# Expert stage of a two-block network: both halves of the tokens in one stationary tile, down weights taken straight from their landing buffer

## What is computed

```
def hierarchical_moe(h, w_rg, b_rg, w_re, b_re, w1, w3, w2):
    ...
    combine = jnp.sum(jax.nn.one_hot(expert_id, N_EXPERTS, dtype=jnp.float32)
                      * weight[..., None], axis=1)
    ...
        hid = jax.nn.silu(jnp.einsum('td,edf->tef', tk, w1)) * jnp.einsum('td,edf->tef', tk, w3)
        hid = hid * c[:, :, None].astype(hid.dtype)
        return jnp.einsum('tef,efd->td', hid, w2)
```

## Time and profile before

| | us |
|---|---|
| median of 3 runs | 1795.31 (1793.7 to 1795.73) |
| the profiled execution | 1794.04 |
| its span in the profile | 1792.0 |
| PE busy in the span | 1533.0 |
| DVE busy | 947.2 |
| ACT busy | 714.4 |
| expert stage, first token tile scaled to the last store's issue | 702.54 to 1062.24 |

### The profile page before, as it was taken

One profiled execution on the slowest core, in us unless ns is written; L12 is line 12 of the kernel. 1 busy time (PEld: TensorE's weight loads), 2 busy tenths in 40 slices (PEclk: granted clock), 3 DMA queues, 4 the chain that ended last, 5 costly groups with the idle time before them and its releaser, 6 DMA issues.

```text
span 1792.0 us, 17556 instructions
## 1 busy us (share of the span) xinstructions
PE 1533.0 (86%) x7159; PEld 1154.2 (64%) x7159; DVE 947.2 (53%) x1295; ACT 714.4 (40%) x1035; POOL 61.9 (3%) x64
## 2 busy tenths in 40 slices
PE   5999998779879954999999965984888798999999
PEld 4888876567547823555555534763877676678887
DVE  3443335834683445788888846745635353321334
ACT  4333143434453212666666643434212136652231
POOL 1000000000000001111111010000000000000000
PEclk9999999979889975999999987986989899999999
DMA  6422321022104323999999963200000222002241
GB/s 200 160 95 83 105 95 53 12 77 76 54 12 144 141 94 113 316 335 331 333 336 334 334 214 125 92 24 0 1 0 1 71 94 94 1 1 71 94 141 47
DMA packets 79179, 219.81 MB, mean 123 GB/s; under 512 B 8899, under 2 KB 10037, under 8 KB 74998
## 3 DMA queue, kind: packets, MB, share of 16 engines
q1 hardware_dynamic: 71670, 193.73, 32.0%
q0 software_dynamic: 4864, 16.52, 2.8%
q10 hardware_dynamic: 2560, 8.39, 1.3%
HBM read 197.91 MB, written 20.71 MB: 122 GB/s over the span
## 4 chain that ended last, share of the span: by engine, by line
PE 61%; DVE 25%; ACT 10%; issue 2%; DMA 1%; SPq 0%; POOL 0%; DVEq 0%; POOLq 0%; ACTq 0%
PE PS L497 15%; PE PS L499 14%; PE PS L498 14%; DVE wlo L1109 6%; DVE htlo L1109 5%; PE PS L892 4%; ACT whi L1881 3%; PE PS L494 2%; DVE ylo L1109 2%; PE PS L1034 2%; ACT yhi L1881 2%; ACT hthi L1881 2%; ACT work L1881 1%; PE PS L1025 1%; DVE work L1506 1%
## 5 line engine op out<-in xcount | busy, mean ns | idle before, releaser
L1109 DVE TENSOR_TENSOR wlo<-raw,whi 128x2048 fp32r<-128x2048 f32 x74 | 169.3, 2291 | 390.0 <-ACT whi L1881 390.0
L1881 ACT ACTIVATE whi<-raw 128x2048 fp32r<-128x2048 f32 x74 | 141.1, 1911 | 385.1 <-PE PS L499 383.7
L494 PE MATMUL PS<-consts,work 128*128 128x128 f32 (+1 forms) x684 | 107.1, 302 | 129.8 <-DVE work L1129 53.6
L497 PE MATMUL PS<-whi,hthi 128*128 128x512 f32 x480 | 192.0, 400 | 20.5 <-ACT work L1881 12.4
L497 PE MATMUL PS<-hthi,whi 128*128 128x512 f32 x480 | 202.7, 422 | 5.4 <-ACT scratch L1881 3.1
L494 PEld LDWEIGHTS PS<-consts,work 128*128 128x128 f32 (+1 forms) x684 | 90.2, 182 | 161.3 <-DVE work L1129 54.8
L499 PE MATMUL PS<-hthi,wlo 128*128 128x512 f32 x480 | 192.1, 400 | 0.0
L498 PE MATMUL PS<-htlo,whi 128*128 128x512 f32 x480 | 191.9, 400 | 0.0
L498 PE MATMUL PS<-wlo,hthi 128*128 128x512 f32 x480 | 190.0, 396 | 0.0
L499 PE MATMUL PS<-whi,htlo 128*128 128x512 f32 x480 | 190.0, 396 | 0.0
L1881 ACT ACTIVATE work<-PS 128x512 f32<-128x512 f32 (+3 forms) x212 | 107.4, 532 | 87.6 <-PE PS L956 54.2
(11 more groups left out here) (316 smaller groups left out, 2589.8 us busy)
## 6 DMA issues: line engine op xcount, KB each, us to landing
raw<-in_w_in SPq DMA_DIRECT2D x44, 1024.0 KB, 5.1
raw<-in_w SPq DMA_DIRECT2D x80, 512.0 KB, 6.1
scratch<-in_w SPq DMA_DIRECT2D x48, 512.0 KB, 6.7
raw<-in_w SPq DMA_DIRECT2D x19, 1024.0 KB, 8.9
scratch<-in_w SPq DMA_DIRECT2D x13, 1024.0 KB, 8.8
raw<-in_w_gate SPq DMA_DIRECT2D x8, 1024.0 KB, 5.0
raw<-in_w_out SPq DMA_DIRECT2D x8, 1024.0 KB, 5.2
y_scratch<-work ACTq DMA_DIRECT2D x32, 256.0 KB, 7.2
```

Of the source, the lines that this page charges most:

```text
L494: return e.transpose(o, i, ident[0:n, 0:n])
L497: e.matmul(o, lh, rh, start=start, stop=False)
L1109: tt(lo, raw_place(j), as_f32(hi), SUB).then_inc(*ve.mark("lo", j))
L1881: return e.activation(o, i, f, bias=bias, scale=scale)
```

## The change

- `up(n)`: the high and low part of the tokens lie side by side in one tile `G` of 128 columns, high in columns 0 to 63 and low in 64 to 127. With it as the stationary operand PE makes 16 matmuls, high weights and low weights in turn, and PSUM gets 128 rows: 64 from the high part, 64 from the low part. ACT copies the lower 64 rows to SBUF (`low_half`), and DVE adds the others (`join`). The sigmoid and the two multiplications read that sum, `UPS`, in SBUF.
- `down(n)`: the hidden values (`HT`, one ACT copy, no low part) and the weights are plain fp32. PE makes 4 matmuls of 512 columns, straight from the landing buffer. The down unit has no split on ACT and DVE, and its landing buffer is free only when PE's `down(n)` is done.
- Buffers: landing buffers go from five to seven; the two new ones are the upper halves of `yhi` and of `ylo`, there under the name `y_plain`. Split pairs go from five to four.
- Order: PE's turn is now `up(n)`, `hand_over(n - 1)`, `bring(n + 1)`, `down(n - 1)`. ACT's turn begins with a split (of the first unit of up(n + 2)), then `hand_over(n - 1)`, `low_half(n)`, `bring(n + 1)`, `gate_hidden(n)`, the second split, `down(n - 1)`. DVE's is split, `bring(n + 1)`, `join(n)`, split, `hidden(n)`.
- Four up units, those of experts 0 and 1, are split before the stage begins; two of these splits lie in the router part.

```
-    LENT_RAW, LENT_SPLIT = 2, 3
+    LENT_RAW, LENT_SPLIT = 4, 2
...
+    whole = {unit["down", n][0] for n in range(NE)}
+    to_split = [j for j in range(UNITS) if j not in whole]
...
         def up(n):
...
-                    m = passes(ps[0:CAP, :], GHI[:, u, kk, :], GLO[:, u, kk, :], wh[:, :, k, :], wl[:, :, k, :],
-                               kk == 0, kk == KD - 1)
+                    e.matmul(ps, G[:, u, kk, :], wh[:, :, k, :], start=kk == 0, stop=False)
+                    m = e.matmul(ps, G[:, u, kk, :], wl[:, :, k, :], start=False, stop=kk == KD - 1)
...
         def down(n):
...
-                on.wait_ge(*ve["lo", j])
-                on.wait_ge(*ve["out", "hidden", n])
+                on.wait_ge(*raw_got[raw_slot[j]][j])
+                on.wait_ge(*ac["out", "hidden", n])
                 for k in range(2):
+                    m = e.matmul(ps[0:CAP, :], HT[:, u, k, :], w[:, k, cols], start=k == 0, stop=k == 1)
...
         bring(0)
         for n in range(NE + 1):
+            if n < NE:
+                up(n)
+            if n:
+                hand_over(n - 1)
             if n + 1 < NE:
                 bring(n + 1)
-            if n:
-                hand_over(n - 1)
-            if n < NE:
-                up(n)
             if n:
                 down(n - 1)
...
+        def low_half(n):
+            u = n % 2
+            on.wait_ge(*pe["up", n])
+            if n > 1:
+                on.wait_ge(*ve["hidden", n - 2])
+            act(UPS[:, u, :], inside("up", n)[CAP:2 * CAP, :], ACT.Copy).then_inc(*ac.mark("low half", n))
...
+        def join(n):
+            u = n % 2
+            on.wait_ge(*ac["low half", n])
+            tt(UPS[:, u, :], UPS[:, u, :], inside("up", n)[0:CAP, :], ADD).then_inc(*ve.mark("out", "up", n))
...
+            elif raw_prior[j] in whole:
+                on.wait_ge(*pe["unit", raw_prior[j]])
```

More of the change, by code:

```diff
@@ L156, in build @@
     htlo = sb("htlo", [P, KD, SEQ], F32R)
+    with nc.sbuf_tensor("y_plain", [P, 2, KD, SEQ], F32) as y_plain:
+        pass
     yhi = sb("yhi", [P, KD, SEQ], F32R)
@@ L748, in hand_over @@
             pv = ps[:, 0:2 * CAP].rearrange("p (k n) -> p k n", k=2)
-            on.wait_ge(*ve["out", "up", n])
+            on.wait_ge(*ve["hidden", n])
             for k in range(2):
@@ L772, in down @@
             u, j = n % 2, unit["down", n][0]
-            wh, wl = (a.rearrange("p (k n) -> p k n", k=2) for a in split_place(j))
+            w = raw_place(j).rearrange("p (k n) -> p k n", k=2)
             for half in range(2):
[L775 to L778, removed]
-                on.wait_ge(*ve["lo", j])
-                on.wait_ge(*ve["out", "hidden", n])
+                cols = slice(half * BANK, half * BANK + BANK)
+                ps = fresh("down", n, half)
+                on.wait_ge(*raw_got[raw_slot[j]][j])
+                on.wait_ge(*ac["out", "hidden", n])
                 for k in range(2):
[L782 to L785, removed]
+                    m = e.matmul(ps[0:CAP, :], HT[:, u, k, :], w[:, k, cols], start=k == 0, stop=k == 1)
+                m.then_inc(*pe.mark("down", n, half))
+                bank.filled(("down", n, half))
             pe.also("unit", j)
@@ L1346, in vector @@
         normalise("n2", g2)
+        split()
         on.wait_ge(*pe["logits"])
@@ L2087, in scalar @@
             split()
-        normalise("n2", g2, lambda i: ve["out", "wo", 1, i])
+        normalise("n2", g2, lambda i: ve["out", "wo", 1, i], [split, split])
         on.wait_ge(*ve["ex"])
@@ L2126, in scalar @@
         bring(0)
-        for _ in range(LENT_SPLIT):
-            split()
         for n in range(NE + 1):
+            if n + 2 < NE:
+                split()
+            if n:
+                hand_over(n - 1)
+            if n < NE:
+                low_half(n)
             if n + 1 < NE:
                 bring(n + 1)
-            if n:
-                hand_over(n - 1)
-            if 2 <= n < NE:
+            if n < NE:
+                gate_hidden(n)
+            if n + 2 < NE:
                 split()
[L2136 to L2141, removed]
             if n:
                 down(n - 1)
+        split()
         ac.also("experts")
@@ L2493, in sync @@
         e.dma_start(xw, xv).then_inc(*xw_got.mark("all"))
-        for j in range(first_out + NR, MOE + NS + NR):
+        for j in range(first_out + NR, MOE + NS + NR + 2):
             load(j)
```

83 lines of the change are left out of this document (43 added, 40 removed).

## The result

The changed kernel takes 1916.87 us (median of 4 runs, 1912.94 to 1919.55), the one before 1795.52 in the same rounds (1793.7 to 1799.03): a ratio of 1.0672, 95% interval 1.0647 to 1.0697. I had forecast slower, but 1822 us and at most 1850.

A forecast was written before the change was run, and what follows sets the result against it. DVE with two hand-overs to ACT bounded the kernel at 10.99 us a turn; a loop through the gated load would make it 12.1. The last store came 27 us later: 1794.0 + 27 = 1821, plus 1.3, 1822 us; range 1792 to 1850.

The forecast's parts named there:

- The new wait: Expert stage: first load of up(n + 2) waits for PE's down(n - 2), closing a loop once per expert.
- Loop A: Expert stage, each turn: gated load's landing, ACT split, `HT`, `down`, hand-overs; 11.1 us at full clock, 12.1 with slow clock.
- L: Landing of the gated pair, two 512 KB DMAs for up(n + 2): taken as 5.0 us, within 4.8 to 6.5.
- Loop B: Expert stage, over two turns through tokens and hidden values: 11.3 to 11.4 us a turn, 11.9 with slow clock.
- The clock: PE in the expert stage: slow spells of 1.6 us in six turns of ten, adding 0.95 us a turn.
- The sum: Whole kernel: 30 turns of 12.1 us, 3 off at first, tail 16.4 after bring(31); last store 27 us later.
- The end of the stage: After the last store: the last split fits into the 4.94 us until results are gathered, costing nothing.
- The first turns: Start of the expert stage: 3 us taken off, as the gated load starts with expert 4's and two units are ready.
- Small prices: Single steps of a turn: `join` 0.69 us, `low_half` half of 1.06, `down` 3.6, two transposes 0.42, `HT` 0.26.
- The traffic or the clock is worse: Rival, expert stage: clock falls every turn, 12.8 us, 1843; or landing takes 6.5 us, 1867; chance 0.19.
- The load isn't waited for: Rival, expert stage: load landed before ACT needs it; ACT and DVE make turns of 10.8 us, 1783; chance 0.13.
- What bounds the kernel before: Expert stage before the change: DVE with two hand-overs to ACT sets 10.99 us a turn; transfers just keep up.

The follow-up runs named there:

- experiment 1: Changed kernel with separate landing buffers, four for up units and three for down units, so no up unit waits for a `down`: 1797.06 us, ratio 1.0004.
- experiment 10: Changed kernel, its seven buffers kept, with ACT's second split moved ahead of the sigmoid: 1909.68 us, ratio 1.063 to the kernel before.
- experiment 4: Changed kernel with SyncE holding back each turn's other three DMAs until the first load pair of up(n + 2) has landed: 1872.46 us, ratio 1.0406.
- Experiment 2: Changed kernel with three unread fp32 products of constants on PE ahead of its wait for `HT`: 1892.61 us, ratio 1.0537 to the kernel before.
- experiment 9: Kernel before with one step moved on ACT, a turn's first split ahead of bring(n + 1): 1760.42 us, ratio 0.9806.
- experiment 6: Changed kernel with separate landing buffers for up and down units and ACT's second split ahead of the sigmoid: 1756.55 us, ratio 0.9787.

## Why the prediction was right in direction and wrong in size

- **The new wait, its place: right.** Loop A, from the end of `down` over the gated pair, ACT's split and `HT` back to `down`, is the whole turn (15.2 us by its parts, 15.2 measured). Experiments 1 and 10 show it from both sides. Loop B never came first.
- **L, taken as 5.0, within 4.8 to 6.5: the first term mis-sized, 7.2.** The argument was that "in a longer turn the former burst is nearly drained when the next begins". That was so, but the gated pair is itself the head of a burst. All five DMAs are issued in 2.5 us, and some 1.4 us of L is their sharing of the engines (experiment 4). The second half's issue, 0.4 us later, I named and did not add to 5.0. The upper bound came from a stage in which loads were issued one by one (6.1), so it was no bound for five at once. 2.2 us a turn.
- **The clock, taken as 0.95 us a turn: the second term mis-sized, 2.2.** I made it from the wait of loop B, 3.3 us without large matmuls, and in six turns of ten. PE's wait for `HT` in loop A itself, up to 4.6 us behind the transposes, I did not count. The clock falls in every turn of the middle and stays low for most of `down`. The Trainium skill, TensorE: Matmul & The Clock Gate (HAM oscillation), has a loop in which every burst behind a long wait starts at the slow clock. The trace agrees for `down` (0.50 from 918 to 924); the `up` right behind a `down` runs at full clock (1.00 at 911). At 12.8 us a turn even that rule, with my price of a spell, stayed short. Experiment 2 holds the clock, and `down` is 3.65. Two slips in the working changed little: 3.4 x (1 - 0.23/0.42) is 1.5 and not 1.6, and the 30 turns before have a seventh slow spell, at 719.8.
- **The sum.** The two terms are 2.2 + 1.25 = 3.4 us over the 12.1 forecast, less 0.3 for the small terms that I had rounded up: 15.2. Thirty such turns are 93 us more than forecast; the last ones, at full clock and with few loads left, gave 4.5 back (bring(31) comes 9.6 us after bring(30)). The tail is 17.7 for 16.4, and the gather comes 2.5 us later behind the last store's issue. That makes the 92 us between my 1819 and the profiled span of 1911.2.
- **The end of the stage: a term put at nothing, 2.5 us.** I let the last split fit into the 4.94 us before the gather. But 2.1 of these follow the last landing, so only 2.8 were free, and ACT's and DVE's split end 4.7 behind the store's issue. In experiment 1, with the store landed in 2.8 us, that costs 1.8. In the changed kernel the store's own landing of 5.3 us ends later still, and sets the 2.5.
- **The first turns: the 3 us came by luck.** The first turn is 11.8 us (712.38 to 724.17), the next 15.4. That is 3.4 under the turn of 15.2, but only 0.3 under the 12.1 of the forecast, from which I had taken 3 off. And it is no gain of early loads: the first turn is 11.8 in experiment 1 too, where the others are 10.95.
- **Small prices right:** `join` 0.68 for 0.69, `low_half` 0.59, `down` 3.65 at full clock for 3.6, two transposes and `HT` as before.
- **The rivals.** "The traffic or the clock is worse" had each half of what happened, the clock in every turn at 1843 or L of 6.5 at 1867, and never both. With both its turn is 6.5 + 6.1 + 1.6 = 14.2 and the time some 1885, outside my range. The two bad ends have one cause, a long wait for the load, so they come together. "The load isn't waited for" had 10.8 us a turn, and experiment 1 has 10.95. Its time is 1797 for 1783: 4 us by the turn, 3 by a gain of the first turns that didn't come, 3 by the tail, 2 by the last split, and 1 by a bring(1) at 713.97.
- **What bounds the kernel before: right, and its floor wrong.** "DVE, with two hand-overs to ACT inside its turn" is shown by experiment 9. That the transfers "just keep up", with 10.4 us at 352 GB/s as "the most that a window here shows", was a rate of demand, not a limit: 9.75 us and 384 GB/s in experiment 6.

## What to carry to other kernels

Before a load is made to wait for the end of the product that it feeds again, draw the closed loop through every queue, count its landing as part of a burst of all that is issued with it, and take long waits and a fallen clock together, not as two independent chances. Give units that are freed by different engines different buffers. And when an even beat goes with small waits on another engine, try to move one instruction in that engine's order before changing what is computed: one moved split gave as much as the whole reworked stage at its best.

## What the runs showed of the hardware that I had not expected

- DMA engines that are 0.98 busy at 334 GB/s can be 1.00 busy at 370 to 384 GB/s with the same loads (the kernel before and experiments 6 and 9). Their busy share says little about what is left.
- The burst shown above, which begins when the transfers rest, moves 16, 152, 274 and 197 GB/s in its first four us (911 to 915), then 152 and 205 in the next two, and some 400 only from the seventh on.
- The time to landing says little about what is waited for: 512 KB take 10.7 us in experiment 6, the fastest of the kernels with the change, where ACT waits 15 us in 240 for landings, and 7.0 in the changed kernel, the slowest, where it waits some 5 us in every turn. What counts is when a load is issued and when ACT comes to it.
